# A different stationary operand for attention times V, in a hybrid attention, convolution and ConvFFN trunk

## What is computed

```python
h = _rmsnorm(x, mix_norm_gain[layer])
q, k, v, conv_in = split(h @ w_in[layer])           # 8 heads of 64
q = _rope(_rmsnorm(q, q_norm_gain[layer]), cos, sin)
k = _rope(_rmsnorm(k, k_norm_gain[layer]), cos, sin)
attn = _dilated_attention(q, k, v)    # 3 causal patterns (window, dilation): (128,1) (512,4) (2048,16)
...
x = x + concatenate([attn, conv]) @ w_out[layer]
```

## Time and profile before

| | us |
|---|---|
| median of 3 runs | 2439.71 (2439.69 to 2440.56) |
| the profiled execution | 2438.82 |
| its span, first to last instruction | 2437.0 |
| TensorE matmul busy | 2406.3 (99%) |
| TensorE weight load busy | 2000.4 (82%) |
| VectorE busy | 1578.7 (65%) |
| ScalarE busy | 792.1 (33%) |

### The profile page before, as it was taken

One profiled execution on the slowest core, in us unless ns is written; L12 is line 12 of the kernel. 1 busy time (PEld: TensorE's weight loads), 2 busy tenths in 40 slices (PEclk: granted clock), 3 DMA queues, 4 the chain that ended last, 5 costly groups with the idle time before them and its releaser, 6 DMA issues.

```text
span 2437.0 us, 30435 instructions
## 1 busy us (share of the span) xinstructions
PE 2406.3 (99%) x11608; PEld 2000.4 (82%) x11608; DVE 1578.7 (65%) x1511; ACT 792.1 (33%) x1050; POOL 154.1 (6%) x57
## 2 busy tenths in 40 slices
PE   7999999999999999999999999999999999999999
PEld 6888898888888888888778888988888888888887
DVE  5999885665555555555749998846555655555555
ACT  4322674432222222222332227744322222222221
POOL 0221001100000000000103110011000000000000
PEclk9999999999999999999999999999999999999999
DMA  4324540112111111111112254301211111111111
GB/s 157 89 80 121 124 92 12 49 51 62 35 52 52 52 43 52 43 52 43 43 35 79 78 147 104 79 18 46 67 49 47 37 49 52 52 46 49 45 50 69
DMA packets 45521, 152.37 MB, mean 63 GB/s; under 512 B 7296, under 2 KB 8960, under 8 KB 45440
## 3 DMA queue, kind: packets, MB, share of 16 engines
q1 hardware_dynamic: 44576, 148.88, 21.0%
q10 hardware_dynamic: 864, 2.36, 0.2%
HBM read 129.97 MB, written 21.23 MB: 62 GB/s over the span
## 4 chain that ended last, share of the span: by engine, by line
PE 91%; issue 4%; DVE 3%; ACT 1%; POOLq 0%; DMA 0%; DVEq 0%; POOL 0%; SPq 0%; ACTq 0%
PE mm L416 59%; PE aux L416 20%; PE aux L564 5%; PE mm L528 3%; PE aux L548 3%; PE aux L443 1%; DVE y L1078 1%; PE aux L452 0%; DMA x<-xT 0%; POOLq L1380 0%; DVE x_lo L1020 0%; PE aux L509 0%; DVE w_lo L1008 0%; DVE x_lo L1215 0%; DVE o L1127 0%
## 5 line engine op out<-in xcount | busy, mean ns | idle before, releaser
L416 PE MATMUL mm<-x_hi,w_hi 128*128 128x512 f32 x1952 | 609.3, 393 | 16.1 <-DVE x_lo L1020 11.5
L416 PE MATMUL mm<-x_hi,w_lo 128*128 128x512 f32 x1952 | 604.8, 391 | 0.0
L416 PE MATMUL mm<-x_lo,w_hi 128*128 128x512 f32 x1952 | 604.1, 391 | 0.0
L416 PEld LDWEIGHTS mm<-x_hi,w_hi 128*128 128x128 f32 x1952 | 364.0, 188 | 95.4 <-issue 11.5
L416 PEld LDWEIGHTS mm<-x_lo,w_hi 128*128 128x128 f32 x1952 | 367.0, 188 | 79.5
L416 PEld LDWEIGHTS mm<-x_hi,w_lo 128*128 128x128 f32 x1952 | 366.9, 188 | 79.0
L704 ACT ACTIVATE w_hi<-w_raw 128x1024 fp32r<-128x1024 f32 x154 | 161.9, 1058 | 656.0 <-PE mm L416 458.1
L1078 DVE SCALAR_TENSOR_TENSOR y<-u_pad,cpar,y 128x1024 f32<-128x1024 f32 x240 | 314.0, 1341 | 3.4 <-ACT y L757 2.6
L1014 DVE TENSOR_TENSOR x<-x,aux 128x1024 f32<-128x1024 f32 x176 | 214.7, 1220 | 121.3 <-PE aux L416 110.8
L1008 DVE TENSOR_TENSOR w_lo<-w_raw,w_hi 128x1024 fp32r<-128x1024 f32 x154 | 192.5, 1255 | 54.9 <-ACT w_hi L704 51.1
L1026 DVE TENSOR_TENSOR uv<-mm,rinv 128x1024 f32<-128x1024 f32 x44 | 53.9, 1225 | 220.1 <-PE mm L416 219.9
(11 more groups left out here) (173 smaller groups left out, 3000.6 us busy)
## 6 DMA issues: line engine op xcount, KB each, us to landing
w_raw<-weights SPq DMA_DIRECT2D x188, 512.0 KB, 3.6
qk_scratch<-m SPq DMA_DIRECT2D x64, 128.0 KB, 2.1
qk_scratch<-o SPq DMA_DIRECT2D x64, 128.0 KB, 2.1
x_hi<-qk_scratch SPq DMA_DIRECT2D x32, 256.0 KB, 6.3
q_first<-qk_scratch SPq DMA_DIRECT2D x8, 512.0 KB, 5.0
k_hh_first<-qk_scratch SPq DMA_DIRECT2D x16, 256.0 KB, 6.3
k_ll_first<-qk_scratch SPq DMA_DIRECT2D x16, 256.0 KB, 6.9
x_hi<-qk_scratch SPq DMA_DIRECT2D x8, 512.0 KB, 4.6
```

The source lines that it names most:

```text
L416: last = pe.matmul(acc[:, cols], a, b[:, cols], start=start and n == 0, stop=stop and n == 2)
```

## The change

In the attend step the operands change places: V (128 keys x 64) becomes stationary and pT (128 keys x 128 queries) moves. V fills only 64 of the array's 128 columns, so the even query block of a pair uses columns 0 to 63 and the odd one columns 64 to 127, and their matmuls alternate in the program. The output comes out turned: 64 values of the head on partitions, queries along the columns, with the even block on partitions 0 to 63 and the odd one on 64 to 127. So:
- `attend` is called four times a head for a pair of blocks, at steps 5, 6, 9 and 10 from the head's first (pairs 0, 3, 1, 2), in place of eight times.
- The block order is 0 6 1 7 2 4 3 5. pT is one large tile (blocks 6, 7 and 4, 5) and one small one (0, 1 and 2, 3). The small one lies in the tile cos.
- At step 8h + 11, behind exps, ScalarE copies the head's output from stat_s to o_turned, in the tile sin (`move_out`, 128x512).
- At step 8h + 12 TensorE turns that copy in four transposes into a bank of stat_b (kind "h"), and VectorE's read_out reads that bank. It frees the bank behind a drain.
- The o turns are one step later (23 and 25, then every 16), and the loops have one step more. `out_part` pieces stand at STEPS + 3, STEPS + 5 and the last step.
- Since cos and sin are overwritten, SyncE loads both tables again in the first layer, behind the last head, ahead of the weights from unit 24 on.

```diff
-O_AT = 22
-BLOCKS = (0, 7, 1, 6, 2, 5, 3, 4)
+O_AT = 23
+BLOCKS = (0, 6, 1, 7, 2, 4, 3, 5)
+ATTENDS = ((5, 0), (6, 3), (9, 1), (10, 2))
+LAST_STEP = STEPS + 10
...
+        if n >= 12 and (n - 12) % TB == 0 and n < STEPS + 12:
+            fills.append((n, "h", (n - 12) // TB, None, None))
...
+        pT_large = sb("pT_large", [P, 2 * TB, P], to=attn)
+        pT_small = cos[:].rearrange("p (k q) -> p k q", q=P)
+        o_turned = [sin[:, i * BANK:(i + 1) * BANK] for i in range(2)]
...
+                if l < DEPTH - 1:
+                    sp.wait_ge(step_done, at(l, 4 * HEADS, 4 * HEADS))
+                    sp.wait_ge(o_read, at(l, HEADS, HEADS + 2))
+                    load_rope()
...
+                    elif kind == "h":
+
+                        pe.wait_ge(o_moved, at(l, HEADS, which + 1))
+                        blocks = [o_turned[which % 2][:, i * P:(i + 1) * P] for i in range(4)]
...
-                    out = stat_s[:, hh * BANK + qb * HEAD_DIM:hh * BANK + (qb + 1) * HEAD_DIM]
-                    for kb in range(qb + 1):
-                        last = pe.matmul(out, pT[n % 2][:, kb, :], vp[b][:, kb, hh * HEAD_DIM:(hh + 1) * HEAD_DIM],
-                                         start=kb == 0, stop=kb == qb)
+                    cols = slice(hh * BANK + pair * P, hh * BANK + (pair + 1) * P)
+                    for kb in range(2 * pair + 2):
+                        for half in range(2):
+                            if kb <= 2 * pair + half:
+                                last = pe.matmul(stat_s[half * HEAD_DIM:(half + 1) * HEAD_DIM, cols],
+                                                 vp[b][:, kb, hh * HEAD_DIM:(hh + 1) * HEAD_DIM],
+                                                 pT(h * TB + BLOCKS.index(2 * pair + half))[:, kb, :],
+                                                 start=kb == 0, stop=kb == 2 * pair + half)
                     last.then_inc(step_done, 1)
...
+                def move_out(h):
+
+                    act.wait_ge(step_done, at(l, 4 * HEADS, 4 * h + 4))
+                    act.wait_ge(o_read, at(l, HEADS, h + 1))
+                    act.activation(o_turned[h % 2], stat_s[:, h % 2 * BANK:(h % 2 + 1) * BANK], ACT.Copy
+                                   ).then_inc(o_moved, 1)
...
                     if n < STEPS:
                         exps(n)
+                    if n >= 11 and (n - 11) % TB == 0:
+                        move_out((n - 11) // TB)
...
-                    dve.wait_ge(step_done, at(l, STEPS, (h + 1) * TB))
+                    dve.wait_ge(pt_full, at(l, PT, f + 1))
...
+                    dve.drain().then_inc(pt_read[f % 2], 1)
...
-                    if n >= 11 and (n - 11) % TB == 0:
-                        read_out((n - 11) // TB)
+                    if n >= 12 and (n - 12) % TB == 0:
+                        read_out((n - 12) // TB)
```

More of the change, by code:

```diff
@@ L123, in turn_schedule @@
     fills = []
-    for n in range(STEPS + 9):
+    for n in range(LAST_STEP):
         if 2 <= n < STEPS + 2:
@@ L309, in raw_count, with pT @@
             return (l * (UNITS // 2) + i * (step // 2) + (base // 2 + 1)) * 16
+        def pT(n):
+            buf, qb = (pT_small, pT_large)[n % 2], BLOCKS[n % TB]
+            first = qb if qb % 2 else 0
+            return buf[:, first:first + qb + 1, :]
         def plain(eng):
@@ L362, in load_head, with load_rope @@
                         sp.dma_start(k_ll[b][half, :].bitcast(F32), rows(1, 1)).then_inc(head_loaded[b], 16)
+                def load_rope():
+                    for table, dst in enumerate((sin, cos)):
+                        for h in range(HPT):
+                            sp.dma_start(dst[h * HALF:(h + 1) * HALF, :].rearrange("f (c q) -> f c q", c=HPT),
+                                         rope_scratch[table].rearrange("c f q -> f c q")).then_inc(rope_loaded, 16)
                 if l:
@@ L577, in out_part @@
                         last.then_inc(mm_full, 1)
-                for n in range(STEPS + 9):
-                    if n == STEPS + 2:
+                for n in range(LAST_STEP):
+                    if n == STEPS + 3:
                         pe.wait_ge(o_split, at(l, 2 * PAIRS, 2 * PAIRS - 2))
-                    if n in (STEPS + 2, STEPS + 3):
-                        out_part(0, 0, [n - STEPS - 2], 0)
+                        out_part(0, 0, [0], 0)
+                    if n == STEPS + 5:
+                        out_part(0, 0, [1], 0)
                     if n < STEPS:
@@ L589, in _ @@
                     for f in range(PT):
-                        if FILLS[f][0] == n and FILLS[f][1] == "p":
+                        if FILLS[f][0] == n and FILLS[f][1] in "ph":
                             turn(f)
-                    if 3 <= n < STEPS + 3:
-                        attend(n - 3)
+                    for k, (at_step, _) in enumerate(ATTENDS):
+                        if (n - at_step) % TB == 0 and 0 <= n - at_step < STEPS:
+                            attend((n - at_step) // TB, k)
                     for f in range(PT):
@@ L1225, in read_out @@
                     dve.tensor_tensor(o_nat[:, :, hh * HEAD_DIM:(hh + 1) * HEAD_DIM],
-                                      stat_s[:, hh * BANK:(hh + 1) * BANK].rearrange("p (b c) -> p b c", b=TB),
+                                      stat_b[:, f % 2 * BANK:(f % 2 + 1) * BANK].rearrange("p (b c) -> p b c", b=TB),
                                       row_rec.unsqueeze(2).broadcast_to([P, TB, HEAD_DIM]),
                                       ALU.mult).then_inc(o_read, 1)
+                    dve.drain().then_inc(pt_read[f % 2], 1)
                 step_taps = list(STEP_TAPS)
-                for n in range(STEPS + 9):
+                for n in range(LAST_STEP):
                     if n < STEPS:
```

32 lines of the change are left out of this document (16 added, 16 removed).

## The result

The changed kernel took 2469.65 us (median of 4 runs, 2469.19 to 2470.93), the kernel before on the same chip 2439.7 us. The ratio is 1.0124, with a 95% interval of 1.0107 to 1.0142. The profiled execution took 2470.12 us, its span was 2467.8 us, 30.8 more than that of before. The prediction said 2465 us, in a range of 2438 to 2495, and slower with a chance of 0.74. Both came true. Whether its reasons do is the matter of the rest.

What follows compares the result with a forecast made beforehand. The prediction took TensorE to set the pace, with VectorE 3 us a head behind. It added 14.0 us for the attention stages and 12 us for the clock to 2438.8 us: 2465 us, range 2438 to 2495.

Steps and rivals of the forecast that it cites:

- The attends: TensorE's attends: two column tiles work at the same time, 5.15 us a head with shape changes, in place of 7.54.
- the changes of shape: Entering and leaving the tiled shape at each attend: 0.11 us a change, 0.22 us an attend of a pair.
- The head turn: TensorE's four transposes of the head's output: TensorE idles 1.9 us waiting for ScalarE's `move_out` copy.
- The heads: Attention stage: plain heads 17.34 us against 16.75; heads holding o turns 21.2 against 18.07, VectorE setting their end.
- the term of +14.0 us: Attention stage of both layers: 156.7 us a layer in place of 149.7, 7.0 more each.
- The clock: TensorE's granted clock falls behind half of 14 idle stretches, 1.7 us each: 12 us, bounds 0 and 24.
- Costed at nothing: Second load of the rope tables, covered by weight unit 24's wait for its split: 0 us; uncovered, 3.5 us once.
- Turns taken: Rival at the attends: column tiles take turns, attends cost 3.4 us more a head, 2490 us; chance 0.2.
- The draining of the tiled shape: Rival at the attends: every tiling change drains the array, 0.27 us each way, 0.54 an attend, 2482 us; chance 0.1.
- The covered wait: Rival at the head turn: `move_out` ends before TensorE arrives, no wait or clock falls, 2432 us; chance 0.12.

Runs made afterwards that it cites:

- experiment 1: Changed kernel with each attend's two loops swapped so column tiles no longer alternate, 2496.24 us; the same with products over the whole array, 2499.9 us.
- Experiments 5 to 7: Changed kernel: o turns one step later, 2466.37 us, with early copy 2442.21; plus moved tap 2437.97; early copy, moved tap, o turns earlier and ahead of attends, 2430.16.
- The kernel with the filled wait: Changed kernel with two unused float32 products of 512 columns ahead of seven of a layer's eight head turns on TensorE: 2458.41 us.
- experiment 3: Changed kernel with ScalarE's copy `move_out` moved ahead of the transposed-block copy and the exponential in its step: 2444.84 us.
- the later o turns alone: Changed kernel with the o turns at steps 24 and 26 in place of 23 and 25, loops one step longer: 2466.37 us.
- the tiles in turn: Changed kernel with each attend's loops swapped, all of the even query block's products before the odd one's: 2496.24 us.
- the whole array: Changed kernel with attend loops swapped and half-width products replaced by products on 128 stationary columns, output not the reference's: 2499.9 us.

## Why the prediction was right, point by point

*The attends.* Predicted 5.15 us a head, measured 4.97 from their starts to the next starts, and 5.3 with the 0.09 us by which each starts later. The tiles do work at the same time; experiment 1 shows it, and shows what the prediction had not named, that the order of issue must alternate for it. The Trainium skill's rule that matmuls whose outputs lie in different column groups run concurrently (TensorE: Matmul & The Clock Gate, Part 3: Packing small matmuls) agrees with 1.90 against 3.04 us, in full for this order of issue alone. In the trace the two tiles' instructions start in pairs, 0.007 us apart, with a pair every 0.109 us. The odd block sets the length, so four attends are 4 + 8 + 12 + 16 = 40 times 0.109, 4.36 us, where the prediction had 4.27. The rest is the changes of shape. They come to some 0.25 us an attend by this sum and to 0.28 against the kernel before, where 0.22 was counted: the reason that the prediction gave, a weight load no longer hidden, is what the rows of experiment 1 show (0.17 us idle at each change). The Trainium skill says that changing the tiling mode "drains the TensorE" (TensorEngine Tiling (Array Packing), Key Properties). These rows agree that each change has a price, about half of the 0.54 us that the rival put on it; whether the array is empty by then they do not show.

*The head turn.* Predicted 1.9 us, measured 1.79 in eight of 14 cases, 2.63 in four and 1.65 in two. Taken away, it gave 24.8 us with its clock.

*The heads.* Plain: predicted 17.34, measured 17.62 where the clock held. O head: predicted 21.2, measured 21.36, with splits that wait 0.87 and 2.17 us where 0.98 and 2.28 were predicted. Experiments 5 to 7 show that these waits bear on the o head's length. The kernel with the filled wait shows the layer without the clock's falls: first head 16.6 us (predicted 15.0), plain heads 52.9 (52.0), o heads 62.9 (62.4 with the tap that runs out), from the last b7 mask to the channel sums 21.4 (21.0). That is 3.4 us a layer more than predicted, half of it the first head. There I had added 1.1 us of waits to VectorE's work, and VectorE waits 1.12 and 1.06 us for scores and 0.25 for a turn. So the term of +14.0 us was mis-sized: 18.7 by that kernel's median. It also took 149.7 us as the stage of both layers, though the second took 151.2 with its fall of the clock; set right, the predicted 156.7 us a layer give +12.5.

*The clock.* Predicted 12 us, measured 11.2. The size is right, the rule behind it was not. I took falls behind half of 14 waits, at 1.7 us each. There are three a layer: at both waits of 2.63 us (0.65 and 0.50 over the four microseconds behind them) and at the one of 1.65 in the last head (0.50), none at a wait of 1.79. They cost 1.4, 2.2 and 2.5 us, as these stretches show against the same ones with the wait filled. It was chance that six falls at some 2 us are about seven at 1.7. The half itself came from two waits of 1.57 us in the kernel before, and both stand right behind the split that GpSimd's addition holds up (375.59 to 378.24, the wait until 379.82), a meeting which the changed kernel doesn't have.

*Costed at nothing.* The second load of the rope tables, in the kernel after, on SP's queue, with the split that the weights wait for anyway:

```profile
414.39 1.77 SPq L380 DMA_DIRECT2D sin<-rope_scratch  x4
416.20 1.85 SPq L380 DMA_DIRECT2D cos<-rope_scratch  x4
...
427.72 1.65 DVE L1048 TENSOR_TENSOR w_lo<-w_raw,w_hi 128x1024 fp32r<-128x1024 f32 x1 [0.95 <-ACT w_hi L735]
```

That split comes 10.78 us behind L638 (416.94), as it came 10.77 us behind L607 before (411.47, 400.70). It did cost nothing.

*The rivals.* Turns taken: made to happen, it gives 2496 us, where 2490 was worked out. The draining of the tiled shape is there in kind and at about half the price, so its 2482 us did not come. The covered wait was not what happened, but experiment 3 makes its condition true, and then its price falls short: 2444.8 in place of 2432, because plain heads stop at 16.65 us, not 15.8, at the banks that VectorE lets go late. Why TensorE's saving did not show is thus settled in the main: of 2.5 us a head, none reached the end until ScalarE's copy, VectorE's taps and the o turns were placed for the new pace.

What stays open is when the clock falls. In the profiled executions of four kernels (the changed one, the later o turns alone, the tiles in turn, the whole array) all 18 head-turn waits of 2.63 to 2.88 us had a fall, which began within the wait or in the four microseconds behind it. Of the 32 waits of 1.79 us 11 had one: 0, 4, 4 and 3 of 8 by kernel. Of the six of 1.65 us three had one.

## What to carry to other kernels

When the engine that sets the pace gets less work, look at each hand-over with the next two engines in their written order before counting the saving: here one copy that stood 1.8 us too late in ScalarE's order cost 24.8 us with the clock behind it. Products on two column tiles overlapped in full only when they alternated tile by tile, and each change of shape cost something, so one long tiled group should be cheaper than several short ones (not tried here). Where TensorE must wait some 2 us often, filling the wait with idle products can pay (11.2 us here); taking the wait away paid more (24.8).

## What the hardware showed unexpectedly

- Work that computes nothing made the kernel 11.2 us faster, with the granted clock at 1.00 throughout.
- The clock fell to 0.50 at idle times of TensorE of 1.57 to 2.88 us, and not at each of them.
- VectorE's subtraction of two tiles in SBUF, 0.69 us, took 2.65 us beside GpSimd's addition of 2.35 us. It ended at 378.75, 0.56 us behind GpSimd's end at 378.19, so it seems to have waited for nearly all of it. The Trainium skill says that the two engines share a pair of SBUF ports, locked for a whole instruction, and that the loser "fully blocks" (SBUF - State Buffer, Terms); these rows agree.
- TensorE's weight loads stood idle for 0.17 us at each change between the whole array and the two column tiles.
- Half-width products in turn cost 0.101 us an instruction in the attend of 30, products over the whole array with the same moving columns 0.109 (3.27 us).
